# Odd mixer: the order of weight chunks around the gate products, ScalarE's sigmoids and table loads, and VectorE's last products

## The reference

```python
h = _rmsnorm(x, mix_norm[1])
# _odd_mixer
proj = h @ w_in                                    # 1024 x 2048
gate = gelu(proj[..., :1024], approximate=True)    # "b" chunks
u = depthwise_conv4(proj[..., 1024:]) + conv_b     # "u" chunks
# _rglru, once per direction, per block of 128 channels
r = sigmoid(u @ w_a + b_a)                         # "r" gate product
i = sigmoid(u @ w_x + b_x)                         # "i" gate product
log_a = -8 * r * softplus(-lam)
a = exp(log_a)
b = sqrt(-expm1(2 * log_a)) * (i * u)
hs = scan(h_t = a_t * h_(t-1) + b_t)               # forward, and reversed
x = x + ((hs_forward + hs_reverse) * gate) @ w_out # "o" chunks
x = x + _swiglu(_rmsnorm(x, ffn_norm[1]), ...)
```

## Time and profile before

| | |
|---|---|
| median of three runs | 1343.62 us |
| profiled execution, time | 1345.33 us |
| profiled execution, span from first to last instruction | 1343.6 us |
| TensorE matmul busy | 1300.5 us, 97% |
| VectorE, ScalarE, GpSimd busy | 544.7, 540.4, 655.5 us |
| mean granted TensorE clock | 0.992 |
| odd mixer, first to last chunk | 778.1 to 972.5 us of the span |

### The profile page before, as it was taken

How to read it: one execution, slowest core, us unless ns; L and a number is a source line. 1 busy time by engine, 2 the same in 40 slices (tenths; PEclk the granted TensorE clock), 3 DMA queues, 4 the chain that set the end, 5 groups by cost and what they waited for, 6 DMA issues and landing times.

```text
span 1343.6 us, 18486 instructions
## 1 busy us (share of the span) xinstructions
PE 1300.5 (97%) x6561; PEld 1038.0 (77%) x6561; DVE 544.7 (41%) x844; ACT 540.4 (40%) x995; POOL 655.5 (49%) x529
## 2 busy tenths in 40 slices
PE   8999999999999999999999988897999999999998
PEld 6877777777778888888888865666788888888886
DVE  4466575655644412121202055987661212121021
ACT  4354444444434433233323235775343323333223
POOL 3465564546535444444444433657344444444442
PEclk9999999999999999999999999998999999999999
DMA  5522221222314333333323232224223333333332
GB/s 175 177 72 63 59 71 57 58 65 60 122 52 118 86 102 93 102 94 96 101 94 100 94 126 63 87 87 141 79 79 102 95 101 94 97 115 96 101 94 94
DMA packets 123543, 126.31 MB, mean 94 GB/s; under 512 B 8024, under 2 KB 106584, under 8 KB 122840
## 3 DMA queue, kind: packets, MB, share of 16 engines
q1 hardware_dynamic: 123448, 125.46, 31.0%
q10 hardware_dynamic: 32, 0.01, 0.0%
HBM read 119.15 MB, written 6.29 MB: 93 GB/s over the span
## 4 chain that ended last, share of the span: by engine, by line
PE 56%; issue 21%; POOL 11%; DVE 6%; ACT 3%; DMA 1%; POOLq 0%; SPq 0%; DVEq 0%; ACTq 0%
PE ps L1402 16%; PE ps L1404 15%; PE ps L1403 15%; POOL w_lo L501 11%; PE ps L1809 2%; PE ps L1530 1%; DMA w_stage<-in_odd_w_in_dram 1%; PE ps L1565 1%; PE ps L1542 1%; PE ps L1546 1%; PE ps L1507 1%; POOL rot L510 1%; DVE gelu_g L1361 1%; PE ps L1576 1%; ACT r_g L837 1%
## 5 line engine op out<-in xcount | busy, mean ns | idle before, releaser
L501 POOL TENSOR_TENSOR w_lo<-w_stage,w_hi 128x512 fp32r<-128x512 f32 (+2 forms) x448 | 565.0, 1265 | 664.9 <-ACT w_hi L574 664.5
L574 ACT ACTIVATE w_hi<-w_stage 128x512 fp32r<-128x512 f32 (+2 forms) x448 | 265.8, 596 | 659.9 <-PE ps L1404 624.5
L1402 PE MATMUL ps<-h_hi,w_hi 128*128 128x512 f32 x1104 | 440.8, 399 | 3.5 <-DVE h_lo L936 1.2
L1404 PE MATMUL ps<-h_hi,w_lo 128*128 128x512 f32 x1104 | 430.2, 390 | 0.0
L1403 PE MATMUL ps<-h_lo,w_hi 128*128 128x512 f32 x1104 | 430.1, 390 | 0.0
L1402 PEld LDWEIGHTS ps<-h_hi,w_hi 128*128 128x128 f32 x1104 | 207.3, 188 | 65.8 <-issue 16.0
L1404 PEld LDWEIGHTS ps<-h_hi,w_lo 128*128 128x128 f32 x1104 | 207.2, 188 | 43.9
L1403 PEld LDWEIGHTS ps<-h_lo,w_hi 128*128 128x128 f32 x1104 | 207.5, 188 | 42.4 <-issue 2.4
L1255 DVE TENSOR_TENSOR silu_g<-ps,rstd_wide 128x512 f32<-128x512 f32 x44 | 30.2, 687 | 327.3 <-PE ps L1404 327.3
L1402 PE MATMUL ps<-w_hi,f_hi 128*128 128x512 f32 x176 | 68.6, 390 | 0.1
L1403 PE MATMUL ps<-w_lo,f_hi 128*128 128x512 f32 x176 | 68.5, 389 | 0.0
(11 more groups left out here) (218 smaller groups left out, 1656.0 us busy)
## 6 DMA issues: line engine op xcount, KB each, us to landing
w_stage<-in_ffn_w_gate_up_dram SPq DMA_DIRECT2D x176, 256.0 KB, 3.1
w_stage<-in_ffn_w_down_dram SPq DMA_DIRECT2D x88, 256.0 KB, 2.7
w_stage<-in_even_w_in_dram SPq DMA_DIRECT2D x96, 192.0 KB, 2.5
w_stage<-in_odd_w_in_dram SPq DMA_DIRECT2D x32, 256.0 KB, 2.9
x_spill<-x_t SPq DMA_DIRECT2D x2, 2048.0 KB, 7.6
x_t<-x_spill SPq DMA_DIRECT2D x2, 2048.0 KB, 7.9
w_stage<-in_odd_w_out_dram SPq DMA_DIRECT2D x16, 256.0 KB, 2.7
w_stage<-in_even_w_out_dram SPq DMA_DIRECT2D x16, 192.0 KB, 2.4
```

What stands on the lines that cost most here:

```text
L501: pool.tensor_tensor(out=w_lo[:, s, 0:n], in0=stage[:, s, 0:n], in1=w_hi[:, s, 0:n].bitcast(f32), op=ALU.subtract).then_inc(chunk_lo, 1)
L574: act.activation(w_hi[:, j % RING, 0:n], stage[:, j % RING, 0:n], ACT.Copy).then_inc(chunk_hi, 1)
L1402: pe.matmul(out_, lh, rh, start=start, stop=False, skip_group_check=skip)
L1404: return pe.matmul(out_, ll, rh, start=False, stop=stop, skip_group_check=skip)
```

## The change

In `ODD`, ("i", m) now follows ("r", m) after four plain chunks instead of two, and ("r", m+1) follows ("i", m) after two instead of four; the output chunks 4 to 7 of both halves alternate in pairs. ScalarE takes the sigmoids and tanhs of r ahead of the conversion that stands in the same slot (index 8(m+1)), roots and decays move ahead of the i sigmoids for m = 0 to 2, the gelus are placed anew, and a small sigmoid of one column behind them brings the sigmoid table back. The norm's sum, root and spread stand earlier, with the root table loaded ahead of a conversion. VectorE does `gate_in(1)`, `gate_in(2)` and `gated(4, 6)` inside a `recur`, and `gated(0, 4)` ahead of `gate_in(3)`. GpSimd's i*u follow one chunk later.

```diff
 ODD = (two_tiles("u", *range(8)) +
-       [("r", 0)] + two_tiles("u", 8, 9) + [("i", 0)] + two_tiles("u", 10, 11, 12, 13) +
+       [("r", 0)] + two_tiles("u", 8, 9, 10, 11) + [("i", 0)] + two_tiles("u", 12, 13) +
...
-       [("o0", k) for k in range(4, 8)] + [("o1", k) for k in range(4, 8)])
+       [("o0", 4), ("o0", 5), ("o1", 4), ("o1", 5), ("o0", 6), ("o0", 7), ("o1", 6), ("o1", 7)])
...
                 for m in range(4):
                     at_ = ODD.index(("i", m))
-                    if j in (at_ + 5, at_ + 6):
-                        driven(m, 2 * (j - at_ - 5))
-                        driven(m, 2 * (j - at_ - 5) + 1)
+                    if j in (at_ + 4, at_ + 5):
+                        driven(m, 2 * (j - at_ - 4))
+                        driven(m, 2 * (j - at_ - 4) + 1)
...
+                elif n == 2:
+                    square(n, 4, 6, gain)
+                    conv(c0 + 4)
+                    square(n, 6, 7, gain)
+                    conv(c0 + 5)
+                    square(n, 7, 8, gain)
+                    act.activation(scratch[:, 6:7], ones[:, 0:1], ACT.Sqrt)
+                    conv(c0 + 6)
+                    root(n)
+                    act.activation(scratch[:, 4:5], ones[:, 0:1], ACT.Sigmoid)
+                    convs(c0 + 7, c0 + 9)
+                    return
...
                     at_ = 8 * (m + 1)
-                    if j == at_ + 1:
+                    if j == at_:
                         sigmoids(m, 0)
-                    if j == at_ + 2:
                         tanhs(m)
-                    if j == at_ + 4:
+                    if j == at_ + 5:
                         sigmoids(m, 1)
-                    if j == at_ + 5:
+                    if j == at_ + (6 if m == 3 else 2):
                         roots(m)
-                    if j in (at_ + 6, at_ + 7):
-                        decays(m, 2 * (j - at_ - 6))
-                if j in (31, 40):
-                    for n in range(4):
-                        gelu((4 if j == 40 else 0) + n)
-                if j in (53, 54):
-                    square(3, 2 * (j - 53), 2 * (j - 52), G_FFN + 8)
+                    if j == at_ + (7 if m == 3 else 3):
+                        decays(m)
+                if j == 33:
+                    gelus(0, 4)
+                    act.activation(scratch[:, 5:6], ones[:, 0:1], ACT.Sigmoid)
+                if j in (40, 41):
+                    gelus(2 * j - 76, 2 * j - 74)
+                if j in (54, 55):
+                    square(3, 2 * (j - 54), 2 * (j - 53), G_FFN + 8)
                 conv(C_ODD + j + RING)
...
+                    if t == 4 and between is not None:
+                        between()
...
-            recur(1)
-            gate_in(1)
-            recur(2)
-            gate_in(2)
-            gate_in(3)
+            recur(1, lambda: gate_in(1))
+            recur(2, lambda: gate_in(2))
             gated(0, 2)
             gated(2, 4)
-            recur(3)
-            gated(4, 6)
+            gate_in(3)
+            recur(3, lambda: gated(4, 6))
             gated(6, 8)
...
+                if (stage_, k) == ("u0", 3):
+                    norm_sum(2, 6)
                 if (stage_, k) == ("u1", 0):
-                    norm_sum(2, 6)
-                if (stage_, k) == ("u1", 2):
                     norm_spread(2, 7)
```

More of the change, by code:

```diff
@@ L45 @@
 ODD = (two_tiles("u", *range(8)) +
[L46 to L49 removed]
+       [("r", 0)] + two_tiles("u", 8, 9, 10, 11) + [("i", 0)] + two_tiles("u", 12, 13) +
+       [("r", 1)] + two_tiles("u", 14, 15) + two_tiles("b", 0, 1) + [("i", 1)] + two_tiles("b", 2, 3) +
+       [("r", 2)] + two_tiles("b", 4, 5, 6, 7) + [("i", 2)] + two_tiles("b", 8, 9) +
+       [("r", 3)] + two_tiles("b", 10, 11, 12, 13) + [("i", 3)] + two_tiles("b", 14, 15) +
        [("o0", k) for k in range(4)] + [("o1", k) for k in range(4)] +
[L51 removed]
+       [("o0", 4), ("o0", 5), ("o1", 4), ("o1", 5), ("o0", 6), ("o0", 7), ("o1", 6), ("o1", 7)])
 ODD_BANK = {"u0": 4, "u1": 2, "u2": 0, "u3": 2, "b0": 0, "b1": 2, "b2": 0, "b3": 2, "o0": 4, "o1": 0}
@@ L245, in build @@
         a_stat, b_stat = at("a_stat", S + 2592, [4, 2]), at("b_stat", S + 2624, [2, 4, 2])
-        scratch = at("scratch", S + 2688, [1])
+        scratch = at("scratch", S + 2688, [8])
         marks = at("marks", S + 2912, [2, 8])
@@ L619, in second_half @@
                 convs(c0 + 6, c0 + 9)
+                act.activation(scratch[:, n:n + 1], ones[:, 0:1], ACT.Sqrt)
                 root(n)
             def root(n):
-                act.activation(scratch[:, :], ones[:, 0:1], ACT.Sqrt)
                 act.wait_ge(norm_ms, n)
@@ L635, in _ @@
             act.wait_ge(ones_set, 1)
-            act.activation(scratch[:, :], ones[:, 0:1], ACT.Sqrt)
+            act.activation(scratch[:, 0:1], ones[:, 0:1], ACT.Sqrt)
             for c in range(NC):
@@ L680, in first_pair @@
                     act.activation(rstd_qk[:, :, :, :], rstd_qk[:, :, :, :], ACT.Sqrt).then_inc(qk_sqrt, 1)
-                    act.activation(scratch[:, :], ones[:, 0:1], ACT.Exp)
+                    act.activation(scratch[:, 7:8], ones[:, 0:1], ACT.Exp)
                 if j == 7:
@@ L816, in _, with gelus @@
             second_half(2, G_MIX + 8, C_ODD)
-            def gelu(n):
-                act.wait_ge(gelu_in, n + 1)
-                act.activation(gelu_g[:, n, :], gelu_g[:, n, :], ACT.Gelu_apprx_tanh).then_inc(gelu_done, 1)
+            def gelus(n0, n1):
+                for n in range(n0, n1):
+                    act.wait_ge(gelu_in, n + 1)
+                    act.activation(gelu_g[:, n, :], gelu_g[:, n, :], ACT.Gelu_apprx_tanh).then_inc(gelu_done, 1)
             def tile_of(m, t):
@@ L851, in roots, with decays @@
                     act.activation(m_gs[m % 2][:, t, :], m_gs[m % 2][:, t, :], ACT.Sqrt).then_inc(root_done, 1)
-            def decays(m, t0):
-                for t in (t0, t0 + 1):
+            def decays(m):
+                for t in range(4):
                     n, d = tile_of(m, t)
@@ L1330, in gate_in, with recur @@
                     V.tensor_tensor(gelu_g[:, 2 * g + q, :], ps[:, ODD_BANK[f"b{g}"] + q, :], rstd_wide[:, :], ALU.mult).then_inc(gelu_in, 1)
-            def recur(m):
+            def recur(m, between=None):
                 r_g, i_g, a_g, m_g = r_gs[m % 2], i_gs[m % 2], a_gs[m % 2], m_gs[m % 2]
```

2 lines of the change are left out of this document (1 added, 1 removed).

## The result

The change makes the kernel faster by 0.9%, about half of what was forecast.

The account below looks back on a forecast made before the run. TensorE bounds it (matmuls busy 97%), so its idle and slow-clock time can be won. 30.4 + 0.4 - 1.5 - 1.6 - 1.5 = 26.2, taken as 25.5 us: median 1318 us, range 1312 to 1330.

Parts of the forecast that it names:

- The norm part: Norm ahead of r0: early root table and earlier sum remove r0's 3.74 us wait, 1.78 slow clock, 0.4 small waits.
- The i3 and gelu step: Last gate: four gelus and two table loads ahead of i3's mark finish just in time; no loss, at most 2 us.
- The seam: After the output: alternating pairs leave less slack before the second half's start; 1.5 us lost, bounds 0 and 4.5.
- GpSimd then has low, i*u twice, low, i*u twice, low in a row: Each cycle, counted from an r product's end (R): seven GpSimd operations take 11.0 us; 1.5 us lost over three cycles.
- rival 2: GpSimd's low parts and i*u take 2.1 us each, losing up to 4 us per cycle, 1332 us; chance 0.09.
- rival 4: Low parts starved by VectorE's unbroken rows; decides from a mean GpSimd operation of 3.05 us; 1353 at 3.3; chance 0.03.
- The output: Output chunks: VectorE's earlier start leaves two short s_lo waits, 1.6 us, replacing 3.24 + 1.65; 8.47 and its 1.65 go.
- rival 1: VectorE becomes the bound of the output; 5 to 8 us are given back, 1325 us; chance 0.17.
- The check by the other sum: VectorE's work from u2's eviction ends at 927.5 without waits, 934 with its new waits; last output pair at 933.6.

Follow-up runs that it names:

- iu_left_out: The changed kernel with GpSimd's products i*u left out, a one-column write in place of each: 1316.64 us, ratio 0.9788 to the kernel before.
- iu_on_vector: The changed kernel with all sixteen products i*u moved from GpSimd to VectorE: 1327.09 us, ratio 0.987 to the kernel before.
- iu_halved: The changed kernel with two of four i*u per gate on GpSimd, one per chunk, and two on VectorE: 1324.78 us, ratio 0.9865.
- iu_on_vector_gaps: The changed kernel with all i*u on VectorE, each recurrence operation also waiting for the one ahead of it: 1330.58 us, ratio 0.9905.

## Why the gain was half of the forecast

*What held.* The waits of the earlier trace rows for r_g and "issue" went in full. The norm part was put at 6.5 us (R0 = 806.9) and gave 7.0 (806.40), although its sum waits 1.1 us for the last squares, which was not priced. The forecast's total counted only 5.9 us for it (3.74 + 1.78 + 0.4). No i product waits; the sigmoids start as r ends, and an undisturbed cycle is 23.20 us for 23.7. The i3 and gelu step cost nothing, as forecast. The seam waits 0.98 us for 1.5.

*The step "GpSimd then has low, i*u twice, low, i*u twice, low in a row": mis-sized.* The burst starts at R + 18.5 (forecast R + 18.3) and TensorE wants its last low part at R + 28.7 (R + 28.8), both right. In the first two cycles it takes 12.5 and 12.8 us and not 11.0; in the third it takes 10.9, and there the wait is 0.80 us, near the 0.5 forecast. The i*u take what they were priced at (24.9 us for sixteen, 1.55 each, for 1.54). What the medians missed is the low parts: the two long bursts open with one of 2.80 and 3.14 us, held off by VectorE's row of operations, the third with one of 1.28. The forecast cost was 1.5 us; measured are 5.3 of waits and 2.0 of slow clock, **5.8 us more**. This is rival 2 at a smaller size, with rival 4's mechanism in the first low part.

*The step "The output": two terms wrong.* It has recur(2) end near 892 and recur(3) begin near 905.3; they came at 900.7 and 918.05, 12.7 us later. First, the 892 lacks the forecast's own waits. From u2's eviction to the end of recur(2) the kernel before has 72.2 us of work (830.02 to 903.46, less 1.24 idle), with gate_in(2) some 73.4, and 817.7 + 73.4 is 891; the 7 us of idle time that the same paragraph expects of VectorE are not in it. VectorE did wait, 5.7 us, all of it for i*u. Second, the work was taken at its old pace: up to there it took 77.6 us (817.34 to 900.71, less 5.74 idle), and gated(0, 4) took 16.1 us instead of 12. With its 7 us in place the forecast would have had the first s_lo some 4 us behind TensorE (an estimate: 898 and half of the 12 us, for 899), and the wait of 3.68 us that it had at nothing would have been on the list. Forecast were 1.6 us of waits and no slow clock; measured are 6.2 of waits and 1.8 + 1.9 of slow clock, **8.3 us more**. This is rival 1. The check by the other sum (934 against 933.6) did not catch it: 109.8 us of work end at the s_lo of the fifth output chunk, before gated(6, 8), so the two ends that agree are not the same operation.

*The account.* The terms added up to 26.2 us before 0.7 was taken off. 26.2 - 5.8 (burst) - 8.3 (output) + 1.1 (norm) + 0.5 (seam) = 13.7 us, against 13.8 between the spans; the medians are 12.2 apart. The forecast priced rivals 1 and 2 one at a time, and its range reached to most of rival 2; they came together, and it had no case for both.

*One cause for both.* The forecast treated the two shortfalls as separate rivals, but iu_left_out takes both away with one edit (but for a single wait). That the cause is the sixteen i*u on GpSimd is shown by this. How much of it is the shared pace of the two engines, how much VectorE's 5.7 us of waiting for i*u and how much GpSimd's queue is argued from rows: the same 108 VectorE operations are busy for 23.3 us less without i*u, and spreading the burst takes the cycle waits away but not the total. VectorE's recurrence moved forward by 16.6 us and i*u by 2.9, so that i*u now runs beside the recurrence and no longer beside the convolution. The forecast had the times of both moves in hand and did not lay them side by side. The Trainium skill, page "SBUF — State Buffer", section "Who interferes with whom", calls the port pair that VectorE and GpSimd share an exclusive lock and says that "Issue order, not op shape, decides who blocks." The alternation at 1.7 us agrees. It does not say how long the blocked one can wait: the 7.49 us of one low part beside some ten VectorE operations are several turns lost in a row, and here the measurement decides.

*Rival 4* (low parts starved by unbroken rows) was priced by a mean of 3.05 us. Its mechanism exists: iu_left_out, iu_on_vector and iu_halved have single operations of 7.9, 7.5 and 5.3 us, and in the three kernels with predecessor waits no low part takes over 2.29. The kernel before has one too, of 4.38 us. After the change it acts in small, in the low parts of 2.80 and 3.14 us; as a mean it never came near 3.05.

*Still open.* What decides whether VectorE takes turns or runs through was not isolated: a wait for the operation just ahead ends the run-through, but whether the gap in time or the wait does it was not tried. Why the predecessor waits cost 4.7 to 5.9 us by the ratios was seen only as later s_lo and w_lo, not split into gaps and lost turns. That the low part shut out in iu_left_out is a case of the same was read from its length beside VectorE's rows; no waits were put in there.

## What to carry to other kernels

When work of two engines that share a port is moved so that it runs side by side, lay the new times of both side by side, price the meeting by the rows where they did meet, and price both engines: the lost time showed up once as late weights and once as late products. Put every wait that the forecast names into every time that lies behind it: here 7 us stood in one sum and not in the other. An order in which every engine is just in time has no place for this; look for a split of the moved work over both engines, here two of four products on VectorE, which took the kernel to 0.9865. And a first test that leaves the suspected work out tells within one run whether two shortfalls have one cause.

## What the runs showed of the hardware

- VectorE's operations with two inputs in SBUF start 0.60 us apart at their own pace and 1.7 us apart in turns with GpSimd's, whose own 1.27 us become 1.7 (after, 828.98 on).
- GpSimd can lose several turns in a row: up to 7.91 us (iu_left_out) and 7.49 (iu_on_vector) for an operation of 1.26, beside VectorE operations that don't wait for the one just ahead; 2.29 us at most in iu_on_vector_gaps, where they do.
- A wait of 2.42 us of TensorE was followed by a stretch at the slow level (clock 0.94 over the cycle), one of 2.04 us in the next cycle was not (1.00); in the output a wait of 1.84 us, which began 2.6 us behind a window with a clock of 0.64, was followed by one at 0.65.
